# Request taps of two gate tiles moved from VectorE to GpSimd, with ScalarE's order around the first xbc taps rewritten

## The reference, cut to what matters

```
proj = h @ w_in
a_val, a_gate, z, xbc, dt_raw = split(proj)            # 512, 512, 512, 1024, 8 channels
a_glu  = a_val * sigmoid(a_gate)
a_conv = causal_dwconv(a_glu, conf_state, conf_w, conf_b)   # 31 taps for each channel
a_out  = silu(layernorm(a_conv, ln_g, ln_b))
xbc_c  = silu(causal_dwconv(xbc, ssd_conv_state, xbc_w, xbc_b))   # 4 taps
dt     = softplus(dt_raw + dt_bias)
y      = ssd_scan(xs, dt, a, b_in, c_out, ssd_state)   # xs, b_in, c_out are parts of xbc_c
```

## Time and profile before

| | us |
|---|---|
| median of 3 runs (lowest, highest) | 1727.03 (1726.93, 1727.35) |
| the profiled execution | 1725.18 |
| its span, first to last instruction | 1723.3 |
| PE's mean granted clock in it | 0.997 |

### The profile page before, as it was taken

How to read it: one execution, slowest core, us unless ns; L and a number is a source line. 1 busy time by engine, 2 the same in 40 slices (tenths; PEclk the granted TensorE clock), 3 DMA queues, 4 the chain that set the end, 5 groups by cost and what they waited for, 6 DMA issues and landing times.

```text
span 1723.3 us, 28511 instructions
## 1 busy us (share of the span) xinstructions
PE 1675.9 (97%) x11696; PEld 1589.0 (92%) x11696; DVE 1062.9 (62%) x1709; ACT 718.9 (42%) x1289; POOL 417.9 (24%) x327
## 2 busy tenths in 40 slices
PE   7999888999999999999999999999999999999999
PEld 6989776897999999999989898789799999999999
DVE  3899967547677646465654335654666774655564
ACT  4322474244434435253542135533543452534352
POOL 3424321220004233232213033100110241414240
PEclk9999899999999999999999999999999999999999
DMA  8322350142213131303143223503330314122312
GB/s 265 105 94 85 87 196 7 62 197 110 86 37 130 45 132 32 129 25 129 37 130 74 75 74 105 207 27 140 130 105 19 123 48 132 45 73 84 95 59 92
DMA packets 40253, 164.96 MB, mean 96 GB/s; under 512 B 9448, under 2 KB 10344, under 8 KB 26176
## 3 DMA queue, kind: packets, MB, share of 16 engines
q1 hardware_dynamic: 32816, 127.21, 22.2%
q0 software_dynamic: 7312, 35.98, 5.8%
HBM read 152.49 MB, written 10.42 MB: 95 GB/s over the span
## 4 chain that ended last, share of the span: by engine, by line
PE 80%; DVE 4%; ACT 1%; issue 1%; POOL 0%; DVEq 0%; ACTq 0%
PE G L991 57%; PE S L991 12%; PE Q L991 11%; PE Q L1717 1%; ACT work L1813 0%; DVE ev_low L2724 0%; DVE stats L2754 0%; DVE resid L3006 0%; ACT h_split L1813 0%; PE Q L1429 0%; DVE stats L3125 0%; DVE work L2767 0%; ACT front L1813 0%; DVE w_split L2979 0%; ACT rstd L1813 0%
## 5 line engine op out<-in xcount | busy, mean ns | idle before, releaser
L991 PE MATMUL G<-ffn_rows,w_split 128*128 128x320 f32 x2160 | 329.8, 309 | 0.0
L991 PEld LDWEIGHTS G<-ffn_rows,w_split 128*128 128x128 f32 x2160 | 320.1, 188 | 0.0
L1813 ACT ACTIVATE w_split<-ring 128x512 fp32r<-128x512 f32 (+2 forms) x224 | 159.1, 711 | 316.5 <-PE G L991 208.1
L907 POOL TENSOR_TENSOR mkT<-ring 128x512 f32<-128x512 f32 x72 | 98.0, 1365 | 564.7 <-DMA ring<-in_w_up 383.7
L991 PE MATMUL G<-h_split,w_split 128*128 128x320 f32 x1344 | 200.9, 310 | 1.2 <-DVE w_split L2484 0.9
L991 PEld LDWEIGHTS G<-h_split,w_split 128*128 128x128 f32 x1344 | 197.5, 188 | 1.9 <-issue 1.3
L991 PE MATMUL G<-g_split,w_split 128*128 128x320 f32 x1056 | 163.7, 310 | 0.1
L991 PEld LDWEIGHTS G<-g_split,w_split 128*128 128x128 f32 x1056 | 156.7, 188 | 1.6 <-DVE w_split L2979 1.4
L2846 DVE TENSOR_TENSOR w_split<-ring,w_split 128x512 fp32r<-128x512 f32 (+1 forms) x124 | 104.8, 846 | 60.6 <-ACT w_split L1813 59.4
L2979 DVE TENSOR_TENSOR w_split<-ring,w_split 128x512 fp32r<-128x512 f32 (+1 forms) x80 | 66.4, 830 | 115.1 <-ACT w_split L1813 114.3
L2568 DVE SCALAR_TENSOR_TENSOR S<-front,par,S 128x512 f32<-128x512 f32 x232 | 107.0, 545 | 0.1
(11 more groups left out here) (365 smaller groups left out, 3265.5 us busy)
## 6 DMA issues: line engine op xcount, KB each, us to landing
ring<-in_w_up SPq DMA_DIRECT2D x44, 1024.0 KB, 4.8
ring<-in_w_down SPq DMA_DIRECT2D x48, 256.0 KB, 2.6
ring<-in_w_down SPq DMA_DIRECT2D x32, 320.0 KB, 2.9
front<-in_mem_k POOLq DMA_DIRECT2D x8, 1024.0 KB, 7.0
front<-in_mem_v POOLq DMA_DIRECT2D x8, 1024.0 KB, 11.1
resid<-in_x SPq DMA_DIRECT2D x8, 640.0 KB, 9.3
ring<-in_w_mk SPq DMA_DIRECT2D x4, 1024.0 KB, 5.9
ring<-in_w_mv SPq DMA_DIRECT2D x4, 1024.0 KB, 10.8
```

Source lines behind the costliest of these rows:

```text
L907: nc.gpsimd.tensor_tensor(wsum[n], a, b, ALU.subtract).then_inc(sum_ready, 1)
L991: return nc.tensor.matmul(out, lhsT, rhs, start=start, stop=stop, **kw)
L1813: return nc.scalar.activation(*a, **k)
```

## The change

GpSimd gets `step_taps(j, batch)`: the request taps of gate tiles 2 and 3 in eight batches of up to four taps. The four taps of a batch are written to four separate rows, and each batch after the first is added to the rows of the first in one pass of 512 elements; two last additions fold the four rows into `acc`. Gate tile 2's first four batches stand ahead of POOL's `memory_keys(1)`, its other four behind it; gate tile 3's eight batches stand around `front_low(10)` to `front_low(13)`. On DVE the prompt taps of gate tiles 2 and 3 run in turn, `gate_rows(3)` and `step_sizes` stand at other places among the taps, and the sums for the layer norm stand later among the xbc taps. On ACT `xbc_first(0)` and `xbc_first(1)` stand behind `front_high_part(12)` and ahead of `xbc_rows(3)` and `front_high_part(13)`; the mean and the squares stand later. On PE `conv_stat(3)` stands behind tile 15 in place of tile 13. `conv` now counts 186 taps.

```
+        tap_sum, tap_rows = (v.rearrange("p (w t) -> p w t", w=4) for v in (hT, xdt[0]))
...
+        step_tap, step_sum = sem("step_tap"), sem("step_sum")
...
+            tapped = [0]
+
+            def step_taps(j, batch):
+
+                src, first = [padded(aglu, j, 0, CPROMPT, CREQ, w)[1] for w in range(CW)], 4 * batch
+                count = min(4, CW - first)
+                rows = tap_rows if batch else tap_sum
+                if batch == 0:
+                    read_wait(pool, TILE0["glu"] + 2 * j + 1)
+                if tapped[0]:
+                    pool.wait_ge(step_tap, tapped[0])
+                for w in range(count):
+                    ins = nc.gpsimd.tensor_scalar(runs(rows[:, w, :]), src[first + w], pr("cw", j * CW + first + w),
+                                                  pr("cb", j) if first + w == 0 else 0.0, ALU.mult, ALU.add)
+                ins.then_inc(step_tap, 1)
+                tapped[0] += 1
+                if batch:
+                    pool.wait_ge(step_tap, tapped[0])
+                    total = tap_sum[:, 0:count, :]
+                    nc.gpsimd.tensor_tensor(total, total, tap_rows[:, 0:count, :], ALU.add).then_inc(step_tap, 1)
+                    tapped[0] += 1
+                if first + count == CW:
+                    pool.wait_ge(step_tap, tapped[0])
+                    total = tap_sum[:, 0:2, :]
+                    nc.gpsimd.tensor_tensor(total, total, tap_sum[:, 2:4, :], ALU.add).then_inc(step_tap, 1)
+                    tapped[0] += 1
+                    pool.wait_ge(step_tap, tapped[0])
+                    nc.gpsimd.tensor_tensor(acc[:, j, SEQ:T], tap_sum[:, 0, :], tap_sum[:, 1, :], ALU.add)\
+                        .then_inc(step_sum, 1)
+                    pool.wait_ge(step_sum, j - 1)
+
+            for batch in range(4):
+                step_taps(2, batch)
             memory_keys(1)
+            for batch in range(4, 8):
+                step_taps(2, batch)
             for n in range(8, 10):
                 front_low(n)
             for j in range(KD):
+                if j < 4:
+                    step_taps(3, 2 * j)
                 front_low(10 + j)
+                if j < 4:
+                    step_taps(3, 2 * j + 1)
                 if j == 6:
                     pool.wait_ge(early_outs, 16 * EARLY_OUTS)
-                    pool.wait_ge(conv, 8 * CW)
+                    pool.wait_ge(conv, 6 * CW)
+                    pool.wait_ge(step_sum, 2)
                     pool.wait_ge(xbc_done, 1)
                     pool.dma_start(h0T, dram["ssd_state"]).then_inc(state_in, 16)
                 read_wait(pool, xbc_tile(j))
...
             for n in range(8, 18):
                 front_project(n)
-                if n == 13:
+                if n == 15:
                     conv_stat(3)
...
             def xbc_first(j):
 
-                act.wait_ge(conv, 8 * CW)
+                act.wait_ge(conv, 6 * CW)
                 if j >= 2:
                     act.wait_ge(xbc_done, j - 1)
                 read_wait(act, xbc_tile(j))
...
-            for j in range(4):
-                xbc_rows(j)
-                front_high_part(10 + j)
-            for j in range(2):
-                xbc_first(j)
+            def conv_mean():
+
+                r = sums(1)
+                A(r, QF[:, 0:T], ACT.Copy).then_inc(stat_read, 1)
+                act.wait_ge(stat_read, nstat[0])
+                A(r, r, ACT.Copy, scale=1.0 / CONF).then_inc(rstd_ready, 1)
+
+            xbc_rows(0)
+            front_high_part(10)
+            xbc_rows(1)
+            front_high_part(11)
+            xbc_rows(2)
+            front_high_part(12)
+            xbc_first(0)
+            xbc_first(1)
+            xbc_rows(3)
+            front_high_part(13)
             xbc_silu(0)
             xbc_rows(4)
             front_high_part(14)
             xbc_silu(1)
             xbc_rows(5)
             front_high_part(15)
-            r = sums(1)
-            A(r, QF[:, 0:T], ACT.Copy).then_inc(stat_read, 1)
-            act.wait_ge(stat_read, nstat[0])
-            A(r, r, ACT.Copy, scale=1.0 / CONF).then_inc(rstd_ready, 1)
             xbc_silu(2)
             xbc_rows(6)
             front_high_part(16)
+            xbc_silu(3)
+            xbc_rows(7)
+            front_high_part(17)
+            conv_mean()
+            xbc_silu(4)
             act.wait_ge(applied, APPLIED["mean"])
             for k in range(4):
                 square(acc[:, k, :])
-            xbc_rows(7)
-            front_high_part(17)
-            xbc_silu(3)
             z_gate(0)
             front_high_part(18)
-            xbc_silu(4)
+            xbc_silu(5)
             log_exp_table()
             act.wait_ge(cs_ready, 1)
             A(dtb[:, 2, :], dtb[:, 2, :], ACT.Exp, scale=-1.0).then_inc(de_ready, 1)
             nc.scalar.preload_act_table_set("silu_and_others")
             z_gate(1)
             front_high_part(19)
-            xbc_silu(5)
-
+            xbc_silu(6)
+            xbc_silu(7)
             log_exp_table()
             inv_std(1, 1.0 / CONF, eps=1)
...
             A(decay[:, :, :].rearrange("p a b -> p (a b)"), G[n % 2][:, 512:512 + NSEG * NH], ACT.Exp)\
                 .then_inc(read[n % 2], 1)
-            for j in range(6, KD):
-                xbc_silu(j)
             z_gate(2)
             act.wait_ge(h_free, 1)
...
+            tap_at = {}
+
+            def conv_tap(j, w, i):
+
+                part = (S[:, j % 2, :] if j >= 2 else S[:, 0, :], runs(S[:, 1, 0:NS]))[i]
+                out = (acc[:, j, 0:SEQ], runs(acc[:, j, SEQ:T]))[i] if w == CW - 1 else part
+                src = padded(aglu, j, 0, CPROMPT, CREQ, w)[i]
+                tap = pr("cw", j * CW + w)
+                if w == 0:
+                    if j:
+                        dve.wait_ge(conv, max(at for (old, _, _), at in tap_at.items() if old < max(j, 2)))
+                    ins = v.tensor_scalar(out, src, tap, pr("cb", j), ALU.mult, ALU.add)
+                else:
+                    dve.wait_ge(conv, tap_at[j, w - 1, i])
+                    ins = v.scalar_tensor_tensor(out=out, in0=src, scalar=tap, in1=part,
+                                                 op0=ALU.mult, op1=ALU.add)
+                ins.then_inc(conv, 1)
+                tap_at[j, w, i] = len(tap_at) + 1
+
+            def both_taps(j, first, end):
+                for w in range(first, end):
+                    for i in range(2):
+                        conv_tap(j, w, i)
+
+            def gate_rows(j):
+
                 n = TILE0["glu"] + 2 * j
                 read_wait(dve, n)
                 tile_wait(dve, n + 1)
@@ -2581,9 +2634,23 @@
                 v.tensor_tensor(b, runs(tmp[:, j % 2, SEQ:T]), runs(GF[(n + 1) % 2][:, SEQ:T]), ALU.mult)\
                     .then_inc(read[(n + 1) % 2], 1)
                 read_wait(dve, n + 1)
-                conv_taps(32 if j < 3 else 44)
+
+            dve.wait_ge(pads_in, 16 * 12)
+            dve.wait_ge(small_ready, 3)
+            gate_rows(0)
+            both_taps(0, 0, 16)
+            gate_rows(1)
+            both_taps(0, 16, CW)
+            both_taps(1, 0, 1)
+            gate_rows(2)
+            both_taps(1, 1, 14)
+            gate_rows(3)
+            both_taps(1, 14, 18)
             step_sizes()
-            conv_taps(8 * CW - taps_done[0])
+            both_taps(1, 18, CW)
+            for w in range(CW):
+                for j in (2, 3):
+                    conv_tap(j, w, 0)
 
...
-            conv_sum(0, lambda k: dve.wait_ge(conv, 8 * CW), lambda k: acc[:, k, :])
...
             done = 0
             for j in range(KD):
-                if j == 3:
-                    subtract_mean()
                 if j == 4:
                     decay_sums()
+                    dve.wait_ge(conv, 6 * CW)
+                    conv_sum(0, lambda k: k < 2 or dve.wait_ge(step_sum, k - 1), lambda k: acc[:, k, :])
+                if j == 5:
+                    subtract_mean()
+                if j == 7:
                     conv_sum(3, lambda k: dve.wait_ge(sq_ready, 24 + k + 1), lambda k: sq[:, k % 2, :])
                 read_wait(dve, xbc_tile(j))
                 dve.wait_ge(xfirst, j + 1)
```

## The result

The changed kernel takes 1732.96 us (median of 7 runs, 1732.44 to 1733.04), the kernel before 1726.93 us beside it (7 runs, 1725.16 to 1727.35): a ratio of 1.0036 with a 95% interval of 1.0026 to 1.0045, so it is slower by 6.0 us. The profiled execution after took 1732.44 us with a span of 1730.6, 7.3 us more than the span before. The execution profiled before lay 1.75 us under its median and the one after 0.52 us under its own, so the spans differ by about 1.3 us more than the medians do.

The account below looks back on a forecast made before the run. PE, working 97% of the span, was taken as the bound. DVE's saving goes into its wait; tile 18 4.5 us late plus 0.5 for the clock gives +5.0, a median of 1732.0 us, range 1729 to 1738.

Parts of the forecast that it names:

- DVE's saving is spent on a wait: On DVE, 62 taps removed save 16.3 us, but `step_sizes` waits 15.7 us for PE's dt tile; taps end at 183.1.
- POOL: Added GpSimd work: 62 taps at 0.35 us and 14 sums at 1.27, a batch 2.9, some 41 us in all.
- Rival 1: GpSimd's taps are dear: from 0.46 us a tap, POOL is late for low part 13; around 1737, chance 0.2.
- Hidden waits: PE waits 2 us ahead of tile 8 and 2.8 ahead of tile 12, costing nothing because tile 13 comes later.
- Rival 3: No loss, the dt tile being there early enough; 1725 with no DVE wait at all; chance 0.04.
- Tile 13: On PE, tile 13 starts at 189.8 after 7.5 us idle, charged with 2.0 us of low clock.
- The chain to tile 18: From tile 15's end at 212.9, a serial chain of 22.5 us makes tile 18 start at 235.5, +4.5 us.
- The clock: Charge of 0.5 us for a clock fall in PE's 5 us of idle behind tile 15, up to 2.0 possible.
- Rival 2: No clock fall ahead of tile 13, or a chain from 212.9 shorter by a microsecond or two: 1729 to 1730.4; chance 0.22.
- Rival 4: POOL's sums stop DVE's convolution taps, moving the taps' end by 14 us: 1746; chance 0.03.

Follow-up runs that it names:

- square of medians: Changed kernel with all GpSimd taps 1732.96 us, with 24 of 31 left out 1732.67; `step_sizes` behind four more tap pairs: 1728.55 and 1718.01.
- few taps: Changed kernel with 24 of 31 request taps of each of gate tiles 2 and 3, and the batch sums, left out on GpSimd: 1732.67 us.
- the reordered kernel: Changed kernel, `step_sizes` later, exponent and squares' sum earlier, gate tile 3's request taps on DVE four taps behind, high parts 13, 14 and `conv_sum(0)` earlier: 1721.42 us.

## Why the prediction held, and where its terms were off

- **DVE's saving is spent on a wait.** Forecast: 15.7 us at `step_sizes`, until 128.1, last tap at 183.1. Measured: 15.49, 128.26, 183.2. The square of medians shows the price: 14.7 us with POOL's load out of the way, 4.4 with it.
- **POOL.** Forecast: a tap 0.35, a sum 1.27, a batch 2.9, the first four done at 120.6; measured 0.36, 1.27, 2.88 (115.52 to 118.40, the next batch's start) and 121.2. POOL's 42.3 us more of busy time for DVE's 14.9 less stand against the forecast's 41 for 16.3. The Trainium skill, "GPSIMD Engine Reference", section "Engine selection", has GpSimd at about half VectorE's speed for two inputs and near line rate for one. The trace agrees for two inputs: a GpSimd sum of 512 columns took 1.27 us, and a DVE sum of 640 took 0.88 (two in 1.76 at 212.41), an estimated 0.70 for 512. The factor here is higher, 42.3 for 14.9, because DVE's tap of 0.26 us is product and sum in one, and GpSimd needs a product of 0.36 and its share of a sum. Rival 1 falls: a tap is under 0.46, and POOL waits 2.96 us ahead of `front_low(13)`.
- **Hidden waits.** PE waits 2.56 and 2.26 us ahead of tiles 8 and 12, forecast 2.0 and 2.8, and with few taps the time stays: their cost was nothing, as the prediction put it, and their cover was the wait at tile 13. With the cover gone POOL's load costs 10.5 us. Rival 3 fell with the 15.49 us of wait; it had priced the case without the wait at 1725, and the run with `step_sizes` later came to 1728.55. It let tile 13 follow tile 12 without a gap, though the prediction itself has POOL free only at 182.5 and a low part takes 2.5: in that run PE waits 2.60 us for POOL at tile 13 and 0.78 at tile 14.
- **Tile 13.** Forecast 189.8 behind 7.5 us of idle, measured 189.96 behind 5.30, since tile 12 started later (177.37 in place of 175.2). That came from tile 8, which the prediction had at the full clock: it ran at 0.52 for 3.3 us. Low part 10, which waits for tile 8's end, and POOL's batches behind it came later: it starts at 155.54, against 153.88 in the run with the exponent early, whose tile 8 kept the full clock. It cost nothing under the wait at tile 13. There the clock fell as charged, if for less: 21 matmuls in 4.7 us against 18 before.
- **The chain to tile 18.** Forecast 235.5, measured 236.0, but the path was not quite that of the prediction, which let it start at tile 15's end, 212.9, with 3.4 us of slack for DVE's sums. The sums were done at 214.2 and not at 209.5: xbc taps 0 to 3 ended at 199.9 and not at 197, one request tap taking 3.05 us in place of 0.34, and the decays took 11.6 us (199.9 to 211.5) and not 10. So PE waited 1.37 us, and the rest of the chain took 21.8 us and not 22.5. That the two errors nearly cancel is luck. The runs with tile 13's high part first show that the chain begins at the taps' end, on DVE, and not at tile 15; that with the exponent early shows that its second half, on ACT, is real.
- **The clock.** 0.5 us was charged for a second fall, and 2.3 measured, tile 18 at 0.50. This is the term that was mis-sized: the sum was +5.0 and the spans differ by 7.3. That the median still came within 1 us of the forecast is luck too: the forecast put it 1.85 us above the profiled execution, and it lay 0.52 above. The run with the exponent early shows it as a term of its own, since there tile 18 keeps the full clock. Rival 2 falls: the clock fell at both places, and from tile 15's end (212.9) to tile 18 the chain took 23.1 us, not a microsecond or two less than 22.5.
- **Rival 4** falls for the convolution's taps: 58 of them from 143.60 took 38.27 us, 0.66 each, as forecast, with POOL busy for 30.76 us of these 38.2 by the stretch's row:

```profile
143.60:181.80 38.20, 34.61 (x222) 34.17 (x223) 38.20 (x60) 6.26 (x14) 30.76 (x45) 0.96 0.32 108
```

## What to carry to other kernels

Work taken from the engine that sets the end can be worth nothing while the next instruction on that engine waits for a producer that hasn't moved; look up when that producer is done before the saving is booked. When a load goes to a helper engine, look at what is queued behind it there: its waits cost nothing as long as a longer one covers them, and their price appears when that one is removed. For a chain over several engines, follow it back from its end through every queue, since a gap that is filled on one engine only moves to the next station if another engine sets the pace.

## What the runs showed of the hardware

A GpSimd pass of 128 partitions by 128 columns in runs of 16, one input, took 0.36 us, 0.12 less than the 0.48 of 256 elements.

DVE instructions with their inputs in SBUF were held up where GpSimd worked at the same time, in amounts that I had not expected: a request xbc tap 3.05 us in place of 0.34 (others beside a low part only 0.73 and 0.69), and the 8-partition operation of the decays 4.18 us in the run with `step_sizes` later against 0.80 in the changed kernel. The Trainium skill, "GPSIMD Engine Reference", section "Specifications", has the two engines share interfaces, in conflict with instructions of two SBUF inputs; these rows agree.

The granted clock fell behind 3.23 and 0.31 us of idle ahead of tile 18, with 0.50 for the next 4.8 us, and behind 3.20 us in the reordered kernel (2.50 us for four matmuls). Behind two waits a tile apart it went both ways: 2.26 and 2.30 us ahead of tiles 12 and 13 brought it down where the high part of tile 13 stands first (0.84 us for tile 13's first two matmuls), 2.25 and 2.26 us did not in the run that differs from it only by DVE's order behind the taps (0.53). At tile 8 it went both ways as well, in kernels whose orders are the same up to there: 0.52 for 3.3 us behind 2.56 us of idle in the changed kernel, 1.00 behind 2.51 us in the one with the exponent early:

```profile
145.80:149.10 3.30, 3.30 (x25) 3.30 (x24) 3.30 (x6) 0.00 (x0) 2.70 (x5) 1.00 0.90 377
```

Which gap brings a fall stays open.
